# A transformer block pair on one core: attention's values taken by quads of heads, modulation summed by transposes

## What is computed

```
mod = silu(c) @ w_mod + b_mod          # 6 x 1024 values; for the context 2 x 1024 more
h = x * (1 + scale1) + shift1
proj = h @ w_in + b_in                 # queries, keys, values of A and B, gate logits
o_a = windowed attention with sink     # 8 heads, 2 key-value heads, 128 wide window + 256 context keys
o_b = global attention                 # 8 heads, 2 key-value heads, 512 + 256 context keys
y = (g_a * (o_a @ w_branch_a) + g_b * (o_b @ w_branch_b)) @ w_out
```

## Time and profile before

| what | value |
|---|---|
| median of 3 runs | 1764.65 us (1764.06 to 1764.79) |
| the profiled execution's own time | 1763.86 us |
| its span | 1762.1 us |
| TensorE busy | 1729.1 us, 98% of the span |
| VectorE, ScalarE, GpSimd busy | 54%, 39%, 47% |
| the chain that ended last | TensorE 95%, VectorE 2%, ScalarE 1% |
| granted TensorE clock over the span | 0.997 |

### The profile page before, as it was taken

How to read it: one execution, slowest core, us unless ns; L and a number is a source line. 1 busy time by engine, 2 the same in 40 slices (tenths; PEclk the granted TensorE clock), 3 DMA queues, 4 the chain that set the end, 5 groups by cost and what they waited for, 6 DMA issues and landing times.

```text
span 1762.1 us, 25819 instructions
## 1 busy us (share of the span) xinstructions
PE 1729.1 (98%) x8687; PEld 1440.9 (82%) x8687; DVE 959.3 (54%) x1613; ACT 681.0 (39%) x1439; POOL 828.7 (47%) x668
## 2 busy tenths in 40 slices
PE   8999999999999999999999999989999999999997
PEld 6888888888877888888888888777788988888887
DVE  4256535667985466252124439376668573551544
ACT  5322221343476423223223223666642642332333
POOL 4554454567982455444444545300044565554551
PEclk9999999999999999999999999999999999999998
DMA  7354452534211446433423333200023134323321
GB/s 231 110 177 146 143 156 83 174 97 126 73 48 49 131 132 191 149 91 96 123 85 92 112 96 95 61 1 1 1 78 90 49 110 141 96 84 108 95 84 49
DMA packets 279716, 178.51 MB, mean 101 GB/s; under 512 B 6280, under 2 KB 258372, under 8 KB 279492
## 3 DMA queue, kind: packets, MB, share of 16 engines
q1 hardware_dynamic: 265364, 149.35, 29.2%
q10 hardware_dynamic: 14256, 27.90, 4.5%
HBM read 175.14 MB, written 2.10 MB: 101 GB/s over the span
## 4 chain that ended last, share of the span: by engine, by line
PE 95%; DVE 2%; ACT 1%; issue 1%; POOL 0%; DMA 0%; DVEq 0%; ACTq 0%; POOLq 0%
PE ps L800 92%; PE ps L1282 2%; DVE actL L2039 0%; POOL wL L680 0%; PE ps L1422 0%; DMA const<-in_const 0%; PE ps L1449 0%; PE ps L980 0%; DVE qB L2517 0%; PE ps L919 0%; POOL actL L734 0%; DVE qA L2517 0%; DVE x L2035 0%; ACT qA L1799 0%; DVE work L2287 0%
## 5 line engine op out<-in xcount | busy, mean ns | idle before, releaser
L680 POOL TENSOR_TENSOR wL<-raw,wH 128x512 fp32r<-128x512 f32 (+2 forms) x560 | 747.6, 1358 | 875.9 <-ACT wH L1554 865.3
L800 PE MATMUL ps<-actH,wH 128*128 128x512 f32 (+1 forms) x1312 | 509.9, 389 | 4.4 <-POOL actL L734 1.9
L800 PE MATMUL ps<-actL,wH 128*128 128x512 f32 (+1 forms) x1312 | 503.9, 384 | 0.4 <-DVE actL L2039 0.4
L800 PE MATMUL ps<-actH,wL 128*128 128x512 f32 (+1 forms) x1312 | 503.6, 384 | 0.0
L1554 ACT ACTIVATE wH<-raw 128x512 fp32r<-128x512 f32 (+2 forms) x558 | 311.6, 608 | 330.4 <-PE ps L800 330.4
L800 PEld LDWEIGHTS ps<-actH,wH 128*128 128x128 f32 x1312 | 246.6, 188 | 55.3 <-ACT wH L1585 2.3
L800 PEld LDWEIGHTS ps<-actL,wH 128*128 128x128 f32 x1312 | 246.7, 188 | 49.7 <-DVE actL L2039 0.8
L800 PEld LDWEIGHTS ps<-actH,wL 128*128 128x128 f32 x1312 | 246.4, 188 | 49.0
L800 PE MATMUL ps<-hidH,wH 128*128 128x512 f32 (+1 forms) x720 | 267.7, 372 | 0.0
L800 PE MATMUL ps<-hidH,wL 128*128 128x512 f32 (+1 forms) x720 | 266.6, 370 | 0.0
L800 PE MATMUL ps<-hidL,wH 128*128 128x512 f32 (+1 forms) x720 | 266.5, 370 | 0.0
(11 more groups left out here) (359 smaller groups left out, 1998.4 us busy)
## 6 DMA issues: line engine op xcount, KB each, us to landing
mod_raw<-in_w_mod ACTq DMA_DIRECT2D x24, 1024.0 KB, 6.4
raw<-in_w_in SPq DMA_DIRECT2D x48, 512.0 KB, 3.7
raw<-in_ffn_w_up SPq DMA_DIRECT2D x44, 512.0 KB, 3.8
raw<-in_w_up SPq DMA_DIRECT2D x44, 512.0 KB, 3.8
raw<-in_ffn_w_gate SPq DMA_DIRECT2D x43, 512.0 KB, 3.9
raw<-in_ffn_w_down SPq DMA_DIRECT2D x32, 512.0 KB, 4.0
raw<-in_w_out SPq DMA_DIRECT2D x16, 512.0 KB, 3.9
raw<-in_w_down SPq DMA_DIRECT2D x16, 512.0 KB, 4.0
```

The costliest lines, as they stand in the source:

```text
L680: nc.gpsimd.tensor_tensor(wL[:, b:b + w // 2], raw[:, b:b + w // 2], wH[:, b:b + w // 2].bitcast(F32), ALU.subtract).then_inc(lo_ready, 1)
L800: return nc.tensor.matmul(out, a, b, start=first, stop=last)
```

## The change

- **Values by quads.** The heads of a tile are taken in the order 0, 1, 4, 5, 2, 3, 6, 7. A quad holds two heads of either key-value head. Behind the first turn of the next quad, `quad_values` takes all its values: for each block one product in the lower column half for the pair of the first key-value head and one in the upper half for the other. So the result stands in bank 6 as features x tokens, and no sum of halves, no turn to tokens and no turn back is needed. `pair_values`, `pair_natural`, `out_T`, `halves` and the 32 transposes go.
- **Normalising.** The reciprocals of the row sums are formed by VectorE at the quad's last unit (`inverse`). Four fp32 products on TensorE, with a column of them repeated 64 times as weights and the identity as moving operand, spread them over the other half of bank 6. VectorE copies that to `inv_rows` and multiplies bank 6 by it into `attnT`.
- **High and low parts.** ScalarE rounds `attnT` into `actH` during B (`HIGHS_AT`: A's four whole tiles, then B's quads), GpSimd subtracts in place into `attnL`. Slots 2 and 3 of the merge's weights are split at units 43 and 45.
- **Buffers.** Turned probabilities have three buffers for two. Query turns go through bank 7 for bank 6.
- **Merge.** Its order is other, and its weight rows are paired like the heads: four DMAs of 64 partitions a slab for two of 128.
- **Modulation.** `mod_acc` is transposed block by block into bank 6 (the context's into bank 7), and VectorE reduces each bank over its columns before it adds the bias.

```diff
-    probT2 = [at("probT2_0", ("stats", 0), 6 * 2 * P), at("probT2_1", ("high", 2 * SLAB), 6 * 2 * P)]
-    out_T = at("out_T", ("high", 2 * SLAB + 6 * 2 * P), 2 * 2 * P)
+    probT2A = [at("probT2A0", ("stats", 0), 1280), at("probT2A1", ("high", 2 * SLAB + 640), 1280),
+               at("probT2A2", ("low", 2 * SLAB + 640), 1280)]
+    probT2B = [at("probT2B0", ("stats", 0), 1536), at("probT2B1", ("kv", 0), 1536),
+               at("probT2B2", ("free", 8 * S + 3 * 768), 1536)]
...
+    inv_rows = sb("inv_rows", 2 * P)
+    attnT = at("attnT", ("free", 0), 8 * S)
+    attnL = at("attnL", ("free", 0), 8 * S, F32R)
...
+    QUAD_HEADS = (0, 1, 4, 5, 2, 3, 6, 7)
...
-    TURN_BANK = [4, 5, 6, 7, 4] + 6 * [6]
+    TURN_BANK = [4, 5, 6, 7, 4] + 6 * [7]
...
+    HIGHS_AT = {35: ("tile", 0), 37: ("tile", 1), 39: ("tile", 2), 41: ("tile", 3),
+                **{4 * quad + 6: ("quad", quad) for quad in range(8, 16)}}
+    HIGHS = [HIGHS_AT[u] for u in sorted(HIGHS_AT)]
+    SPLIT_AT = {43: 2, 45: 3}
...
-                    pool.wait_ge(prob_T, 2 * len(group1))
-                    lows(st, 0, slots=(2, 3))
+                    for n, piece in enumerate(HIGHS):
+                        if piece == ("quad", 10):
+                            lows(st, 0, slots=(2, 3))
+                        pool.wait_ge(attn_high, n + 1)
+                        G.tensor_tensor(attended(attnL, *piece), attended(attnT, *piece),
+                                        attended(actH, *piece).bitcast(F32), ALU.subtract).then_inc(attn_low, 1)
...
-                mm = product(ps[:, 6, q:q + 1], mod_acc[:, q * P:(q + 1) * P], one[:, 0:1], True, True)
+                mm = nc.tensor.transpose(bank(6 + q // 4, P, q % 4 * P), mod_acc[:, q * P:(q + 1) * P], ident)
...
-        def pair_values(i):
-            n = len(group1) + 2 * i + 1
-            values = group2[2 * i]["v"], group2[2 * i + 1]["v"]
+        def quad_values(quad):
+            n, pairs = len(group1) + 4 * quad + 3, (2 * quad, 2 * quad + 1)
+            values = [group2[2 * i]["v"] for i in pairs]
             pe.wait_ge(probT_a, n + 1)
             pe.wait_ge(probT_v, V_TURNS[n + 1])
-            if i > 0:
-                pe.wait_ge(pair_out, i)
-            pe.wait_ge(q2_lo, parts_before(2 * i + 2))
-            for b, v in enumerate(values[0]):
-                half = (lower, upper)[b % 2]
-                mm = product(ps[half, 6, 0:256], v, probT2[i % 2][:, b * 256:(b + 1) * 256],
-                             b < 2, b >= len(values[0]) - 2)
-            mm.then_inc(pair_pv, 1)
-        def pair_natural(i):
-            pe.wait_ge(pair_out, i + 1)
-            if i == 0:
-                pe.wait_ge(q2_lo, parts_to(3, 1))
-            elif i % 2 == 0:
-                pe.wait_ge(attn_out, GROUPS1 + i // 2)
+            if quad == 0:
+                pe.wait_ge(q2_lo, parts_to(2, 1))
+            else:
+                pe.wait_ge(attn_out, GROUPS1 + quad)
+            for b in range(len(values[0])):
+                for half, v, i in zip((lower, upper), values, pairs):
+                    product(ps[half, 6, 0:256], v[b], probT_of(i)[:, b * 256:(b + 1) * 256], b == 0, b == len(v) - 1)
+            pe.wait_ge(inverted, quad + 1)
+            a = 96 + (quad * 4) % 32
             for m in range(2):
-                mm = product(bank(7, DH, (i % 2 * 2 + m) * DH), out_T[:, (i % 2 * 2 + m) * P:][:, 0:P], cv("halves"), True, True)
-            mm.then_inc(pair_nat, 1)
+                for n, half in enumerate((lower, upper)):
+                    mm = product(ps[half, 6, 256 + m * P:][:, 0:P], stat[:, a + 2 * n + m:][:, 0:1].broadcast_to([P, DH]),
+                                 ident, True, True)
+            mm.then_inc(quad_pv, 1)
 
         def second_attention():
             for u in range(len(group2)):
                 if u + 2 < len(group2):
                     logits2(u + 2)
                 turn(len(group1) + u)
-                if u % 2 == 0 and u >= 2:
-                    pair_values(u // 2 - 1)
-                if u % 2 == 1 and u >= 3:
-                    pair_natural(u // 2 - 1)
+                if u % 4 == 0 and u >= 4:
+                    quad_values(u // 4 - 1)
                 if u in TURN_AT:
-                    pe.wait_ge(pair_out, u // 2)
                     turn2(TURN_AT[u])
...
-        pairs, merge_base = len(group2) // 2, stage_of["merge"]["base"]
+        merge_base = stage_of["merge"]["base"]
         pe.wait_ge(logit, len(group1) + len(group2))
-        pe.wait_ge(attn_out, GROUPS1 + QUADS2 // 2)
-        for k in range(4):
-            attended(k, range(ST)).then_inc(at_T, 1)
-        pair_values(pairs - 1)
-        pe.wait_ge(attn_out, GROUPS1 + QUADS2 - 1)
-        for k in range(4, 6):
-            attended(k, range(ST)).then_inc(at_T, 1)
-        pe.wait_ge(lo_ready, (merge_base + 1) * 2)
-        merge_part(0, range(2))
-        pair_natural(pairs - 1)
-        attended(6, range(ST - 1))
-        merge_part(0, range(2, 4))
-        pe.wait_ge(attn_out, GROUPS1 + QUADS2)
-        attended(6, (ST - 1,)).then_inc(at_T, 1)
-        attended(7, range(ST)).then_inc(at_T, 1)
-        pe.wait_ge(lo_ready, (merge_base + 2) * 2)
+        pe.wait_ge(lo_ready, (merge_base + 4) * 2)
+        merge_part(0, range(4))
+        quad_values(QUADS2 - 1)
         merge_part(1, range(4))
-        merge_part(0, range(4, KT)).then_inc(slab_done, 1)
-        merge_part(1, range(4, KT)).then_inc(slab_done, 1)
-        for j in (2, 3):
-            pe.wait_ge(lo_ready, (merge_base + j + 1) * 2)
-            merge_part(j, range(KT)).then_inc(slab_done, 1)
+        for j in range(SLOTS):
+            merge_part(j, range(4, KT)).then_inc(slab_done, 1)
+            if j + 2 < SLOTS:
+                merge_part(j + 2, range(4))
...
-        def pair_drained(i):
-            act.wait_ge(pair_pv, i + 1)
-            if i >= 2:
-                act.wait_ge(pair_nat, i - 1)
-            nc.scalar.activation(out_T[:, i % 2 * 256:][:, 0:256], bank(6, 256), ACT.Copy).then_inc(pair_out, 1)
+        def attended_high(what, n):
+            act.wait_ge(attn_out, GROUPS1 + (QUADS2 // 2 if what == "tile" else n + 1))
+            act.wait_ge(att_qk, len(group1) + len(group2) // 2)
+            nc.scalar.activation(attended(actH, what, n), attended(attnT, what, n), ACT.Copy).then_inc(attn_high, 1)
 
         def second_attention():
             def copy(u):
                 n = len(group1) + u
                 w = BY_ACT[n]
                 act.wait_ge(prob_T, n + 1)
-                if u >= 4:
-                    act.wait_ge(pair_pv, u // 2 - 1)
+                if u >= 6:
+                    act.wait_ge(quad_pv, (u // 2 - 3) // 2 + 1)
                 nc.scalar.activation(turned_into(u, 0, w), bank(4, w * P).rearrange("p (b s) -> p b s", s=P),
                                      ACT.Copy).then_inc(probT_a, 1)
 
...
                 if u + 1 < len(group2):
                     exps(len(group1) + u + 1)
                 copy(u)
-                if u % 2 == 0 and u >= 2:
-                    pair_drained(u // 2 - 1)
                 if u == 0:
                     act.wait_ge(slab_done, stage_of["merge"]["base"])
                     nc.scalar.activation(tile(gates, 15), bank(3), ACT.Identity, bias=col("b_gate", 15)).then_inc(drained_a, 1)
                 for piece in PARTS_AT.get(u, ()):
                     turned_high(*piece)
-                if u % 4 == 3 and group2[u]["sink"]:
+                if u % 4 == 2 and group2[u]["sink"]:
                     sink_terms(u // 4)
+                if u in HIGHS_AT:
+                    attended_high(*HIGHS_AT[u])
+                if u in SPLIT_AT:
+                    split(stage_of["merge"], 0, SPLIT_AT[u])
...
         def mod_columns(chunk, ctx_too):
             dve.wait_ge(mod_sum, chunk + 1)
-            b = cols[:, bass.ds(chunk * 4 + VEC["b_mod"][1], 4)]
-            if ctx_too:
-                link(V.tensor_tensor(modx[:, bass.ds(chunk * 4, 4)], bank(6, 4, 4), b, ALU.add))
-            V.tensor_tensor(modc[:, bass.ds(chunk * 4, 4)], bank(6, 4), b, ALU.add).then_inc(mod_cols, 1)
+            b, four = cols[:, bass.ds(chunk * 4 + VEC["b_mod"][1], 4)], bass.ds(chunk * 4, 4)
+            for into, turned in ((modx, 7), (modc, 6))[0 if ctx_too else 1:]:
+                sums = into[:, four]
+                link(V.tensor_reduce(sums, bank(turned).rearrange("p (m s) -> p m s", s=P), AX_X, ALU.add))
+                ins = V.tensor_tensor(sums, sums, b, ALU.add)
+                if turned == 7:
+                    link(ins)
+            ins.then_inc(mod_cols, 1)
             dve.wait_ge(mod_cols, chunk + 1)
...
+            def inverse(quad):
+                a = (quad * 4) % 32
                 dve.wait_ge(probs, n0 + quad * 4 + 4)
-                total, inverse = stat[:, 32 + a:32 + a + 4], stat[:, 96 + a:96 + a + 4]
-                if u["sink"]:
+                total = stat[:, 32 + a:32 + a + 4]
+                if quad < QUADS2 // 2:
```

(33 more changed lines are left out.)

92 lines of the change are left out of this document (33 added, 59 removed).

## The result

The changed kernel takes 1773.09 us (median of 5 runs, 1771.16 to 1774.98) against 1764.59 us before (5 runs): ratio 1.0047, 95% interval [1.0037, 1.0058]. The forecast was 1768.7 us in a range from 1760 to 1778, with 0.60 for slower. The sign, the mechanism and the size of most terms came out as forecast; 4.4 us were missing in it. A second set of runs of the same kernel, on another occasion, gave 1773.14 us.

A forecast was written before the change was run, and what follows sets the result against it. TensorE bounds the second attention now; after the change the VectorE-ScalarE loop decides. B +9.7, A +3.6, handoff -2.75, modulation -6.6 give +3.95 us on 1763.86: 1767.8, with the runs' median 0.8 above, 1768.7 us; range 1760 to 1778.

The forecast's parts named there:

- B: Second 32 units of the second attention: from 73.76 to 83.5 us, +9.7 us, a quad growing from 9.62 to 10.80 us.
- A: First 32 units of the second attention: last two quads +2.6 us, the six before net +1, together +3.6 us.
- The loop: In B, copy, masking, exponential and ScalarE's copy let a turn start 3.88 us after the turn two before; it decides from the second turn.
- the block: Behind a quad's first turn, 24 values records plus spreading: 4.78 us to the second turn, while VectorE and ScalarE stand still.
- The spreading: Eight TensorE records per quad that spread the reciprocals over a bank: 0.07 us each, 0.56 in all.
- the rule of the Trainium skill: Weight-load time goes by columns: spreading would cost 0.055 us a record, making the sum about 1.8 us lower.
- The handoff: From attention's last turn to the output projection: 4.05 us beside the merge records instead of 6.8, -2.75 us.
- the 5.7 us of such waits go: In A, values no longer wait for the bank that VectorE empties, which removes 5.7 us of waits.
- Modulation: 64 one-column products become 64 turns of 0.11 us: 7.0 instead of 13.6 us, -6.6 us; VectorE's reductions at nothing.
- The cover of 132 us: VectorE idle for 132 us ahead of the drains, so its 16 reductions cost nothing; without that cover, 11 us.
- modulation gives nothing: Rival 3: reductions delay VectorE's drains in the feed-forward and TensorE waits for banks: 1775 us; chance 0.06.
- The clock: Rival 5: TensorE's clock falls to half, B's work of about 70 us taking up to 70 more; chance 0.02.

## Why the prediction was right, and where it fell short

**The loop** was right in its steps: the intervals of a quad within 0.12 us, the instants behind the second turn within 0.01, the normalising as part of the path (moved away, the fourth interval fell from 2.13 to 1.59), the block as the cause (cut in two and in three, the loss goes). B was 0.7 us too dear, mostly because the block ran in 4.69 instead of 4.78 us. TensorE's idle time before turns was put too high with it, 1.9 us a quad for 1.6, and its busy share too low, 83% for 88%.

**The spreading** at 0.07 a record came out at 0.068. The estimate by the rule of the Trainium skill (TensorE: Matmul & The Clock Gate, section LDWEIGHTS), 0.055, was too low for it, and full-width turns at 0.11 too high; the measurement decides. What sets 0.068 no run shows.

**The handoff** was right, -2.6 against -2.75.

**A** was right in size (+3.3 against +3.6) by a reason that was half wrong. "the 5.7 us of such waits go" held: no values wait for VectorE's low part of qB any more. But the low parts of the turned queries stand in VectorE's queue as before, and now it is its copy that comes late. These are A's three longest stands (PE, idle before, what ended it):

```profile
1146.48 0.63 PE L1317 MATMUL ps<-const,prob2A 128*128 128x128 f32 x4 [2.11 <-DVE probT2A L2384]
...
1157.53 0.74 PE L1317 MATMUL ps<-const,prob2A 128*128 128x128 f32 x5 [2.25 <-DVE probT2A L2384]
...
1178.81 0.74 PE L1317 MATMUL ps<-const,prob2A 128*128 128x128 f32 x5 [2.26 <-DVE probT2A L2384]
```

Before, the longest stand in A was 1.44 us; after, three are over 2.1 us. In the kernel with the block in two the longest is 1.09 us: A won there the 4.7 us worked out and the cost of the fall.

**Modulation** was mis-sized twice. A turn takes 0.099 us, not 0.11 (0.79 us for 8): 7.1 to 7.5 us less in the profiles, where 6.6 was forecast. And "I cost them at nothing" failed for VectorE's 16 reductions: with a reduction ahead of the first drain of a stage, the chain behind it comes 1.2 us late, up to 389 (0.7 are the reduction's own time, the rest is open). The cover of 132 us was counted in the feed-forward's drains; the chain at 389 is in the stage behind them, and it has none. It is the form in small of the rival "modulation gives nothing".

**The clock** was the step that failed, though the time stayed within the range. "The granted clock is 1.00 in A, though TensorE idles there for 8 us, so more idle time need not lower it" took the idle time as a sum. It came in single stands of at most 1.44 us before, and in stands of 2.1 to 2.3 us after, and the clock fell for 3.4 us at a time behind these and also behind shorter ones, three and four times in the two profiled executions. The kernel before is probably not free of it either: one of its executions has a mean clock of 0.995, at 1766.56 us. The rival was priced as one long fall (70 us) with 0.02; the form that came was a few short ones, 1.3 to 1.7 us each. The two misses, three falls (+4.7) and VectorE at 389 (+1.2), with the start's +1.4, are 7.3 us; the other terms together were 1.7 us too high, and the difference is, but for rounding, what lies between 1767.8, the forecast on the profiled execution, and 1773.45. So part of the nearness is luck: terms too dear made up for terms that were missing.

**Small slips in its sums.** 1767.8 and 0.8 are 1768.6, not 1768.7. The interval from the third to the fourth turn is 3.88 - 1.64 = 2.24 us by its own loop, and the line for B takes 2.30. Its chances of faster and same add up to 0.14 and 0.26, where it has 0.15 and 0.25. None of it changes the forecast.

## What to carry over

An engine that is 99% busy can be slowed by gathering its work: if the other engines live from its steps in turn, a block of it is paid twice, once while they stand and once while it waits for them to catch up. Before work is joined, ask for each interval between two handovers which engine would be idle in it, and which instructions of the path can be put into that idle time. Here moving two instructions alone made 8 us slower into 2 us faster, and cutting the block in three, with a fourth buffer, made it 8 us faster. Look at TensorE's idle time by its longest stands too, and not only by its sum.

## What the runs showed of the hardware

The clock of TensorE fell to its lower level (1.2 GHz) for 3.4 us each time, behind stands of 1.0 to 2.3 us. The Trainium skill (TensorE: Matmul & The Clock Gate, section "A second HAM failure mode: psum-queue depth-cycling") tells of a kernel whose frequent small idle times between groups of matmuls made the clock swing. This case's traces agree in that the clock swung although no stand near a fall was longer than 2.3 us. But the frequent small ones of B (three of up to 0.7 us a quad, 1.6 in all) had no fall among them in any profile; the falls came behind the longer, single stands. Of extra products in the gaps it is shown that they left a quad at 10.72 us; that they keep the clock up is not shown, since the profiles without them often lack the same falls, and the medians fell by 0.7 and 1.8 us only, less than the spread of the runs.
